# Forgetting attention of a two-block transformer: a block's output product beside the next block's transposes and scores, and the output projection begun with the last head's first slot

## The reference

```python
def fox_attention(q, k, v, c):          # c: running sum of log forget gates
    def block(args):                    # i: one of 8 blocks of 128 queries
        i, q_i, c_i = args
        s = einsum('bqhd,bkhd->bhqk', q_i, k) * D ** -0.5
        s = s + (c_i[..., :, None] - cT[..., None, :])
        s = where(kpos[None, :] <= qpos[:, None], s, -inf)
        p = softmax(s, axis=-1)
        return einsum('bhqk,bkhd->bqhd', p, v)

def fox_mixer(h, k, v, c, w_in, q_norm, w_out):
    q, z = split(h @ w_in, 2, axis=-1)
    o = fox_attention(rms_norm(q), k, v, c) * silu(z)
    return o @ w_out                    # 8 heads x 128 features -> 1024 features

# second_block: h = h + rms_norm(fox_mixer(...), post_norm)
```

## Time and profile before

| | |
|---|---|
| median of 3 runs | 2844.68 us (2844.63 to 2846.89) |
| profiled execution | 2844.63 us, of which the profile's span is 2842.8 us |
| TensorE matmul busy | 2767.9 us, 97% of the span |
| VectorE, ScalarE, GpSimd busy | 1553.7, 851.0, 1033.5 us |
| mean granted TensorE clock | 0.991 |
| rounds w = 1 to 7 of the attention, one after another | about 69.3 us each |
| round w = 8 and all behind it | from 2704 us to the end |

### The profile page before, as it was taken

One profiled execution on the slowest core, in us unless ns is written; L12 is line 12 of the kernel. 1 busy time (PEld: TensorE's weight loads), 2 busy tenths in 40 slices (PEclk: granted clock), 3 DMA queues, 4 the chain that ended last, 5 costly groups with the idle time before them and its releaser, 6 DMA issues.

```text
span 2842.8 us, 34792 instructions
## 1 busy us (share of the span) xinstructions
PE 2767.9 (97%) x13798; PEld 2234.8 (79%) x13798; DVE 1553.7 (55%) x1968; ACT 851.0 (30%) x1295; POOL 1033.5 (36%) x470
## 2 busy tenths in 40 slices
PE   8999999999999999999999999999997999999997
PEld 6887787768888888888888888888875777777775
DVE  7335652224766655556766666666547444444445
ACT  4322222322100000000144555445534333333332
POOL 4334343234334434434422222222336333333235
PEclk9999999999999999999999999999998999999998
DMA  3112231001111111111222222222222111111114
GB/s 148 31 44 77 95 103 45 30 30 49 42 51 45 46 51 44 52 44 44 85 83 73 70 70 63 69 64 70 63 96 82 38 38 38 43 40 44 38 38 158
DMA packets 99156, 173.04 MB, mean 61 GB/s; under 512 B 30640, under 2 KB 60240, under 8 KB 98896
## 3 DMA queue, kind: packets, MB, share of 16 engines
q1 hardware_dynamic: 91312, 144.92, 15.8%
q10 hardware_dynamic: 7200, 24.19, 2.3%
q0 software_dynamic: 512, 2.07, 0.2%
HBM read 152.21 MB, written 18.94 MB: 60 GB/s over the span
## 4 chain that ended last, share of the span: by engine, by line
PE 90%; DVE 5%; issue 2%; ACT 1%; POOL 1%; DMA 1%; ACTq 0%; DVEq 0%; SPq 0%; POOLq 0%
PE gemm L695 20%; PE gemm L697 20%; PE gemm L696 20%; PE small L696 3%; PE small L697 3%; PE small L695 3%; PE small L868 2%; PE small L1390 2%; PE small L1368 2%; PE small L1378 1%; PE small L1247 1%; PE small L981 1%; PE small L1234 1%; PE gemm L814 1%; PE small L1001 1%
## 5 line engine op out<-in xcount | busy, mean ns | idle before, releaser
L695 PE MATMUL gemm<-h_hi,w_hi 128*128 128x512 f32 x2560 | 1076.4, 420 | 33.4 <-DVE h_lo L2200 12.0
L697 PE MATMUL gemm<-h_hi,w_lo 128*128 128x512 f32 x2560 | 1013.5, 396 | 0.0
L696 PE MATMUL gemm<-h_lo,w_hi 128*128 128x512 f32 x2560 | 1013.2, 396 | 0.0
L569 POOL TENSOR_TENSOR w_hi<-w_raw,unit_col 128x1024 fp32r<-128x1024 f32 x180 | 353.2, 1962 | 1432.5 <-PE gemm L697 1183.9
L695 PEld LDWEIGHTS gemm<-h_hi,w_hi 128*128 128x128 f32 x2560 | 484.5, 189 | 142.5 <-issue 17.2
L697 PEld LDWEIGHTS gemm<-h_hi,w_lo 128*128 128x128 f32 x2560 | 482.3, 188 | 116.3
L696 PEld LDWEIGHTS gemm<-h_lo,w_hi 128*128 128x128 f32 x2560 | 484.8, 189 | 98.6 <-issue 6.2
L578 POOL TENSOR_TENSOR w_lo<-w_raw,w_hi 128x1024 fp32r<-128x1024 f32 x164 | 445.6, 2717 | 17.5 <-DVE w_lo L2356 4.9
L661 POOL TENSOR_TENSOR w_hi<-w_raw,unit_col 128x1024 fp32r<-128x1024 f32 x32 | 60.6, 1893 | 325.9 <-PE gemm L697 325.8
L2464 DVE TENSOR_TENSOR norm<-gemm,norm 128x1024 f32<-128x1024 f32 x44 | 53.9, 1225 | 191.8 <-PE gemm L697 188.1
L2495 DVE TENSOR_TENSOR xres<-small,xres 128x1024 f32<-128x1024 f32 x88 | 107.5, 1221 | 58.0 <-PE small L697 57.9
(11 more groups left out here) (436 smaller groups left out, 3908.2 us busy)
## 6 DMA issues: line engine op xcount, KB each, us to landing
w_raw<-w_stream SPq DMA_DIRECT2D x201, 512.0 KB, 3.3
x_spill<-xres ACTq DMA_DIRECT2D x16, 512.0 KB, 2.6
xres<-x_t SPq DMA_DIRECT2D x8, 512.0 KB, 8.4
xres<-x_t ACTq DMA_DIRECT2D x8, 512.0 KB, 5.2
xres<-g_rows SPq DMA_DIRECT2D x8, 512.0 KB, 3.9
norm<-g_rows SPq DMA_DIRECT2D x8, 512.0 KB, 3.8
mt_plane<-xres SPq DMA_DIRECT2D x8, 512.0 KB, 3.2
xres<-t_plane SPq DMA_DIRECT2D x8, 512.0 KB, 4.6
```

Source lines behind the costliest of these rows:

```text
L569: nc.gpsimd.tensor_tensor(whi[d][:, :, :], raw[s][:, :, :], unit, ALU.mult).then_inc(w_hi_done, 1)
L695: mm(dst, w_hi, a_hi, start=first, stop=False)
L696: mm(dst, w_hi, a_lo, start=False, stop=False)
L697: return mm(dst, w_lo, a_hi, start=False, stop=last)
```

## The change

Three tables of slots are changed; no instruction is added or removed and no wait is changed.

- Scores of q = 1 to 4 are issued one slot earlier (6q - 5), those of q = 5 to 7 stay. `fox_max`, `fox_exp` and `fox_rescale` follow the same function.
- The output product of block q is issued in slot 6q + 7 instead of 6q + 4 for q = 0 to 6, which is the slot of the next block's transposes, ahead of them; q = 7 stays. `fox_gate` moves with it (its first half from slot 22 to 25).
- In round w = 8 the groups of the output projection begin in slot 0 with four (before: two in slot 5), 49 are done after slot 26, and the rest follow evenly. `hi_half(0)` and `half_lo(0)` move from slot 24 to 26, and four of the `lo_part` of heads 3 to 6 from slots 3, 5, 6, 7 to 1, 3, 5, 7.

```diff
-        FO_FROM, FO_TO = 4, 67
+        FO_STEPS = ((0, 4), (26, 49), (67, len(FO_GROUPS)))
...
+        def scores_at(q):
+            return 6 * q - (5 if q <= NB // 2 else 4)
+        def out_at(q):
+            return 6 * q + (7 if q < NB - 1 else 4)
         def fo_groups(s):
-            return len(FO_GROUPS) * min(max(s - FO_FROM, 0), FO_TO - FO_FROM) // (FO_TO - FO_FROM)
+            for (a, first), (b, last) in zip(FO_STEPS, FO_STEPS[1:]):
+                if a <= s <= b:
+                    return first + (last - first) * (s - a) // (b - a)
+            return 0
...
-                        if g >= 0 and q and s == 6 * q - 4:
+                        if g >= 0 and q and s == scores_at(q):
                             fox_scores(g, q)
...
-                        if g >= 0 and s == 6 * q + 4:
+                        if g >= 0 and s == out_at(q):
                             fox_out(g, q)
...
-                        if s in (24, 47):
+                        if s in (26, 47):
                             half_lo(s // 47)
```

More of the change, by code:

```diff
@@ L2097, in _ @@
                     for q in range(NB):
-                        if g >= 0 and q and s == 6 * q - 3:
+                        if g >= 0 and q and s == scores_at(q) + 1:
                             fox_exp(g, q)
-                        if g >= 0 and q == 3 and s == 6 * q - 3:
+                        if g >= 0 and q == 3 and s == scores_at(q) + 1:
                             fox_rescale(g, q)
@@ L3050, in _ @@
                 for s in range(65):
-                    for k, at in enumerate(((FOX - 1, 54), (FOX - 1, 56), (FOX - 1, 57), (FOX, 3), (FOX, 5), (FOX, 6), (FOX, 7))):
+                    for k, at in enumerate(((FOX - 1, 54), (FOX - 1, 56), (FOX - 1, 57), (FOX, 1), (FOX, 3), (FOX, 5), (FOX, 7))):
                         if (w, s) == at:
@@ L3067, in _ @@
                     for q in range(NB):
-                        if g >= 0 and q and s == 6 * q - 4:
+                        if g >= 0 and q and s == scores_at(q):
                             fox_max(g, q)
-                        if g >= 0 and q and s == 6 * q - 2:
+                        if g >= 0 and q and s == scores_at(q) + 2:
                             fox_rescale(g, q)
-                        if g >= 0 and q % 4 == 3 and s == 6 * q + 4:
+                        if g >= 0 and q % 4 == 3 and s == out_at(q):
                             fox_gate(g, q // 4)
```

## The result

The changed kernel takes 2862.99 us (median of 4 runs, 2861.64 to 2865.73), the kernel before 2845.78 us in the same series. The ratio is 1.0061, with a 95% interval of 1.0049 to 1.0073: it is slower by 17 us, where 5 us less were forecast. The profiled execution took 2861.64 us, with a span of 2859.8 us and a mean granted clock of 0.992.

The account below looks back on a forecast made before the run. TensorE, busy for 97% of the span, was taken as the bound, so only its waits could pay. Terms of 3.7 - 1.7 + 1.4 + 1.55 + 0.2 = 5.15 us off 2844.63 us gave 2839.5 us, range 2837.8 to 2842.6.

Parts of the forecast that it names:

- the cost of the moved outputs in rounds 1 to 7: Rounds 1 to 7: moving outputs only joins them with transposes and scores; taken as 0, bounds 7.5 us either way.
- Joints cost nothing: Rounds 1 to 7: 88 joints between small groups of matmuls cost and save nothing, 0 us.
- The slower rival: Rounds 1 to 7: joints cost 0.085 us each, 7.5 us for 88, giving 2847.0 us; chance 0.05.
- Block 1's wait for L2990 stays: Rounds 2 to 7: VectorE's instruction is still caught by GpSimd, so gain 0; bound 2.0 us.
- Start of round 8: TensorE's lost time falls from 5.66 to 2.0 us with the clock staying up: gain 3.7 us.
- The wait at group 49: Round 8, slot 27: a new wait for half_lo(0), behind block 5's maximum: loss 1.7 us.
- The sums: Round 8, half_sums(0): the wait falls from 3.0 to 1.6 us, gain 1.4 us, bounds 0 and 3.0.
- The clock behind them: Round 8, behind the sums: the clock stays at 2.4 GHz, gain 1.55 us; other bound 0.
- the clock still falls: Rival: once in round 8, at the start, slot 27 or behind the sums; 1.5 us each, 2841.0 us; chance 0.34.
- Slots 49 to 51: Round 8: evacuation ahead of the eight loads saves 0.6 us, group 96 waits 0.4 us more: gain 0.2 us.
- the end gives its part back: Rival: slot 49's later loads bound what follows; 3.2 us from the sums on are lost, 2842.7 us; chance 0.07.
- the 5.15 us forecast for round 8: Sum of the gains and losses in round 8: 3.7 - 1.7 + 1.4 + 1.55 + 0.2 us.

Follow-up runs that it names:

- outs46: The changed kernel with the outputs of blocks 4 and 6 back in slots 28 and 40: 2845.87 us, ratio 1.0002 to the kernel before.
- scores_all: The changed kernel with the scores of blocks 5 to 7 also one slot earlier (6q - 5 for all): 2842.52 us, ratio 0.9990 to the kernel before.
- round8_only: The kernel before with the change made in round 8 alone, scores and outputs of heads 0 to 6 in old slots: 2845.98 us, ratio 1.0000.
- loads_first: Changed kernel, all scores at 6q - 5; round 8: out(3) in slot 22, first half's parts in 24, residual loads before slot 49's evacuation: 2839.66 us.
- scores5: The changed kernel with block 5's scores alone one slot earlier (25): 2854.20 us in one run.

## Why the prediction was wrong

**The step that failed** is the cost of the moved outputs in rounds 1 to 7. The prediction says that there "the change only joins outputs, transposes and scores" and takes 0 for it. It priced what was moved and the joints; it did not ask what the outputs had stood in front of. out(6) was moved past the key transposes of slot 41, which wait for block 7's maximum, and out(4) past the end of a weight tile that starts GpSimd. The runs show 1.1 and 1.6 us for these two, in each of seven rounds: 19 us. Round 8 held more steps that failed, named below; they decide between 5 us less and nothing, not the sign of the result.

**Joints cost nothing**: right. outs46 and scores_all have most or all of them and no loss. The slower rival named in the prediction had the sign and the wrong mechanism.

**Block 1's wait for L2990 stays**: right. L3001 takes 1.80 us there now, and the wait is the 0.17 us that it was. The same mechanism, used in the prediction to argue that a gain would not come, made the larger part of the loss four blocks later, where before the rescaling had started 1.1 us ahead of GpSimd's instruction and had ended 0.5 us ahead of it.

**Start of round 8**: right in the profile of the changed kernel, and partly by luck. TensorE:

```profile
2722.93 0.40 PE L708 MATMUL gemm<-h_hi,w_lo 128*128 128x512 f32 x1
...
2726.57 0.51 PE L825 MATMUL gemm<-h_hi,w_hi 128*128 128x512 f32 x1 [1.85 <-DVE head L3077]
...
2727.38 0.40 PE L825 MATMUL gemm<-h_hi,w_hi 128*128 128x512 f32 x1
```

It is free of groups 0 and 1 at 2724.57 and lost 2.0 us, at full clock behind it. Seven other profiles have the same wait of 1.85 us there, and in five of them the clock falls behind it, which costs 1.1 to 1.5 us. So in round8_only:

```profile
2707.80 0.51 PE L825 MATMUL gemm<-h_hi,w_hi 128*128 128x512 f32 x1 [1.85 <-DVE head L3077]
...
2711.61 0.63 PE L825 MATMUL gemm<-h_hi,w_hi 128*128 128x512 f32 x1
2712.03 0.63 PE L828 MATMUL gemm<-h_lo,w_hi 128*128 128x512 f32 x1
```

**The wait at group 49**: right, 1.6 us in the view against 1.7 predicted. **The sums**: right in place, 1.49 us (the bracket below) against 2.85 in the earlier trace rows. **The clock behind them**: wrong in this execution. From 2815.25 to 2818.24 matmuls take 0.43 us; the gap ahead was only 1.5 us and the stretch came all the same:

```profile
2812.82 1.02 PE L840 MATMUL small<-const,norm 128*128 128x1 f32 x8 [1.49 <-DVE norm L3019]
...
2815.25 0.63 PE L825 MATMUL gemm<-h_hi,w_hi 128*128 128x512 f32 x1
...
2818.61 0.40 PE L829 MATMUL gemm<-h_hi,w_lo 128*128 128x512 f32 x1
```

That is one rival of the prediction (the clock still falls, chance 0.34), at its price of 1.5 us. In five of the eight profiles with a wait of 1.49 us at the sums, that of round8_only among them, the clock stays up there, as predicted, and falls elsewhere.

**Slots 49 to 51**: wrong. The prediction let the loads move behind the evacuation and followed who waits for the evacuation, not what the loads run beside. GpSimd and TensorE of the changed kernel:

```profile
2831.61 1.89 POOL L580 TENSOR_TENSOR w_hi<-w_raw,unit_col 128x1024 fp32r<-128x1024 f32 x1 [3.90 <-DMA w_raw<-w_stream]
...
2835.99 0.50 PE L825 MATMUL gemm<-h_hi,w_hi 128*128 128x512 f32 x1 [1.80 <-POOL w_lo L589]
```

A weight tile's load lands late, 3.9 us of waiting for GpSimd, since 4 MB of residual are now under way beside it: a piece of the weights takes up to 9.6 us from issue to landing there, 5.6 before the change. loads_first takes GpSimd's wait away by nothing but the loads' place. The prediction's rival "the end gives its part back" (chance 0.07) named the loads too, but as a bound of the residual's own slabs.

With the clock's 1.5 us and this 1.8 us less, the 5.15 us forecast for round 8 become 1.9; the profile of the changed kernel shows 2.2. It was a good one. In the profile of round8_only the wait for the weight tile is 2.5 us long, and the clock falls twice, at the start of round 8 and behind that wait, as it fell twice before the change. From the last projection to the end it takes 140.0 us, 1.0 more than before, and over ten runs it shows no gain.

## What to carry to other kernels

A filler that is moved is also removed from where it stood: list every wait between its old place and its new one, and every release (of a buffer, a tile, a bank) between them, for it covered the first and delayed the second. If work is taken out from between a producer and its consumer, start the producer earlier; one slot (0.7 us) was enough here, and the same change turned from 0.6% slower to 0.1% faster, and with the first half's low part kept ahead of a maximum to 0.3% faster. In a loop whose rounds repeat this exactly, two instructions that miss each other by half a microsecond in one round miss each other in all of them, and a small shift of one makes them meet in all of them.

## What the runs showed of the hardware

- A VectorE instruction that meets a running GpSimd one by 0.03 us waits it out: 0.62 us became 2.29 us, in every one of seven rounds. Started 0.80 us ahead of it, in scores5, it takes its 0.62 us. The Trainium skill ("GPSIMD Engine Reference", Key points) names the contention for instructions with two SBUF inputs or in a two-port mode; the trace fits it with the instruction ending 0.43 us behind GpSimd's, if this rescaling, which reads one SBUF tensor, runs in such a mode, which no row shows.
- TensorE's clock fell to the 1.2 GHz level in different places of round 8 from profile to profile, one to three times in each. Behind the same wait of 1.85 us at the start it fell in five of eight profiles, behind the same 1.49 us at the sums in three of eight. Behind a late weight tile it fell in the five profiles with a wait of 2.0 to 2.5 us and not in the two with 1.4 and 1.8. A stretch held up to 11 of the large matmuls and cost 1.1 to 2.2 us, mostly 1.5. Single runs of the kernel before lie between 2843.0 and 2848.9 us, but for four above 2856 us; that the clock makes this scatter is likely and not shown. Differences of 1 to 2 us were not decided here.
- Eight loads of 512 KB, issued from 2816.1 us on in the changed kernel, made a weight tile late: GpSimd waited 3.9 us for it, and TensorE, 20 us behind the first issue, 1.8 us. TensorE's wait for that tile is 1.4 to 2.5 us in seven kernels.
